# Low weight parts written over the raw tiles: four shared buffers in place of three raw and three low ones

## The reference, cut to what matters

```python
h = rmsnorm(x, norm_mix[i])
proj = h @ w_in[i]
...
merged = gates[:, :, 0] * y_attn + gates[:, :, 1] * y_conv + gates[:, :, 2] * y_ssm
x = x + merged @ w_mix_o[i]
h = rmsnorm(x, norm_ffn[i])
gt, up = jnp.split(h @ w_ffn_in[i], 2, axis=-1)
x = x + (jax.nn.silu(gt) * up) @ w_ffn_out[i]
```

## Time and profile before

| | |
|---|---|
| median of three runs | 2869.71 us (2868.93 to 2874.04) |
| the profiled execution | 2872.15 us, span 2870.4 us, mean granted TensorE clock 0.934 |
| TensorE matmul busy | 2582.4 us (90%), 12117 instructions |
| VectorE busy | 1469.2 us (51%) |
| ScalarE busy | 1034.8 us (36%) |
| GpSimd busy | 1023.8 us (36%) |
| weight stream queue | 200.96 MB, 21.1% of the DMA engines' time |

### The profile page before, as it was taken

One profiled execution on the slowest core, in us unless ns is written; L12 is line 12 of the kernel. 1 busy time (PEld: TensorE's weight loads), 2 busy tenths in 40 slices (PEclk: granted clock), 3 DMA queues, 4 the chain that ended last, 5 costly groups with the idle time before them and its releaser, 6 DMA issues.

```text
span 2870.4 us, 31814 instructions
## 1 busy us (share of the span) xinstructions
PE 2582.4 (90%) x12117; PEld 2051.8 (71%) x12117; DVE 1469.2 (51%) x2304; ACT 1034.8 (36%) x1674; POOL 1023.8 (36%) x577
## 2 busy tenths in 40 slices
PE   4987999999999998898999999987976888799998
PEld 3776667878888777676878888875744466588887
DVE  7775443443344476643433252345588863554333
ACT  3323663332222422465232222352344563422221
POOL 3212333444444422233444444441222233244443
PEclk9999999999999999899999999997977589799999
DMA  3221222322232322122322222231100001122222
GB/s 132 72 67 41 74 70 77 103 89 96 96 103 83 95 77 57 60 69 68 98 103 99 99 96 96 88 112 66 66 8 1 1 12 55 52 81 97 97 100 81
DMA packets 80135, 217.97 MB, mean 76 GB/s; under 512 B 15728, under 2 KB 25328, under 8 KB 79472
## 3 DMA queue, kind: packets, MB, share of 16 engines
q1 hardware_dynamic: 60912, 200.96, 21.1%
q10 hardware_dynamic: 19072, 14.98, 2.0%
HBM read 207.25 MB, written 2.10 MB: 73 GB/s over the span
## 4 chain that ended last, share of the span: by engine, by line
PE 73%; DVE 20%; ACT 3%; issue 3%; POOL 1%; ACTq 0%; DMA 0%; DVEq 0%
PE psG L836 21%; PE psG L837 21%; PE psG L838 21%; DVE work_m L1668 2%; DVE work_b L1668 2%; DVE tmp L1668 2%; PE psO L1002 2%; DVE stats L1948 1%; DVE b_lo L1668 1%; DVE work_b L1671 1%; DVE work_b L2066 1%; DVE max L2065 1%; DVE b_hi L1679 1%; PE psO L1068 1%; PE psT L946 1%
## 5 line engine op out<-in xcount | busy, mean ns | idle before, releaser
L782 POOL TENSOR_TENSOR w_lo<-w_raw,w_hi 128x1024 fp32r<-128x1024 f32 (+4 forms) x417 | 919.7, 2209 | 1610.8 <-ACT w_hi L1260 1610.8
L836 PE MATMUL psG<-h_hi,w_hi 128*128 128x512 f32 x1944 | 785.6, 404 | 23.3 <-DVE h_lo L1712 17.4
L837 PE MATMUL psG<-h_lo,w_hi 128*128 128x512 f32 x1944 | 769.8, 396 | 0.0
L838 PE MATMUL psG<-h_hi,w_lo 128*128 128x512 f32 x1944 | 767.9, 395 | 0.0
L1260 ACT ACTIVATE w_hi<-w_raw 128x1024 fp32r<-128x1024 f32 (+4 forms) x417 | 404.8, 971 | 532.0 <-PE psG L838 514.5
L836 PEld LDWEIGHTS psG<-h_hi,w_hi 128*128 128x128 f32 x1944 | 373.1, 192 | 126.1 <-issue 33.7
L838 PEld LDWEIGHTS psG<-h_hi,w_lo 128*128 128x128 f32 x1944 | 372.6, 192 | 80.1
L837 PEld LDWEIGHTS psG<-h_lo,w_hi 128*128 128x128 f32 x1944 | 373.2, 192 | 77.6 <-issue 3.0
L1668 DVE TENSOR_TENSOR x<-x,psG 128x512 f32<-128x512 f32 x112 | 77.1, 688 | 432.3 <-PE psG L838 432.3
L836 PE MATMUL psG<-m_hi,w_hi 128*128 128x512 f32 x736 | 287.3, 390 | 1.8 <-DVE m_lo L1668 1.7
L837 PE MATMUL psG<-m_lo,w_hi 128*128 128x512 f32 x736 | 286.4, 389 | 0.0
(11 more groups left out here) (273 smaller groups left out, 2943.0 us busy)
## 6 DMA issues: line engine op xcount, KB each, us to landing
w_raw<-wstream SPq DMA_DIRECT2D x327, 512.0 KB, 3.3
w_raw<-wstream SPq DMA_DIRECT2D x64, 256.0 KB, 2.6
w_raw<-wstream SPq DMA_DIRECT2D x16, 384.0 KB, 3.0
work_b<-work_b ACTq DMA_DIRECT2D x16, 256.0 KB, 4.4
work_b<-cmpw ACTq DMA_DIRECT2D x2, 2048.0 KB, 7.7
x<-xT SPq DMA_DIRECT2D x4, 512.0 KB, 6.3
small_work<-ssmp ACTq DMA_DIRECT2D x8, 256.0 KB, 2.7
outT<-x SPq DMA_DIRECT2D x1, 2048.0 KB, 6.3
```

The lines of the kernel that those rows point to most:

```text
L782: pool.tensor_tensor(lo, w, hi.bitcast(F32), ALU.subtract).then_inc(s_split, 1)
L836: pe.matmul(out, whi, hi, start=(k == 0), stop=False)
L837: pe.matmul(out, whi, lo, start=False, stop=False)
L838: ins = pe.matmul(out, wlo, hi, start=False, stop=(k == K - 1))
```

## The change

The tensor `w_lo` is placed at the address of `w_raw`, and both have four slots. GpSimd subtracts the high part from the raw tile and writes the result over it. SP may load into a slot only when the product that reads the low part there has ended, so its wait goes to `s_job` of product n-4 in place of `s_split` of tile n-3. The high part keeps three slots. The pipeline has 28 KB a partition in place of 36, and all tensors placed after it move down by 8 KB.

```diff
--- before.py
+++ after.py
@@ -50,7 +50,7 @@
 UNITS_SW = 16
 XHEADS = 4
 
-RAW_SLOTS = 3
+RAW_SLOTS = 4
 SPLIT_SLOTS = 3
 GEMM_BANKS = 3
 
@@ -446,9 +446,9 @@
         Bl, _ = place("b_lo", [P, 12, SEQ], F32R)
         R, _ = place("work_m", [P, 2 * KD * SEQ], F32, at=m_at)
         R2, _ = place("work_b", [P, 24 * SEQ], F32, at=b_at)
-        raw, _ = place("w_raw", [P, RAW_SLOTS, 8 * P], F32)
+        raw, raw_at = place("w_raw", [P, RAW_SLOTS, 8 * P], F32)
+        Wl, _ = place("w_lo", [P, RAW_SLOTS, 8, P], F32R, at=raw_at)
         Wh, _ = place("w_hi", [P, SPLIT_SLOTS, 8, P], F32R)
-        Wl, _ = place("w_lo", [P, SPLIT_SLOTS, 8, P], F32R)
         CON, _ = place("consts", [P, CONST_N], F32)
         PAR, _ = place("params", [P, npar], F32)
         sqr, _ = place("squares", [P, 2, SEQ], F32)
@@ -761,7 +761,7 @@
                 sp_eng.dma_start(X[:, 2 * i:2 * i + 2, :], xT[:, 2 * i:2 * i + 2, :]).then_inc(s_x[i], 16)
             for n, (key, K, N, who) in enumerate(weights):
                 if n >= RAW_SLOTS:
-                    sp_eng.wait_ge(s_split, n - RAW_SLOTS + 1)
+                    sp_eng.wait_ge(s_job, n - RAW_SLOTS + 1)
                 src = wstream[offset[key]:offset[key] + K * P * P].rearrange("(p f) -> p f", p=P)
                 sp_eng.dma_start(raw[:, n % RAW_SLOTS, 0:K * P], src).then_inc(s_raw[n % RAW_SLOTS], 16)
                 if n == 1:
@@ -777,7 +777,7 @@
                 key, K, N, who = weights[n]
                 w = raw[:, n % RAW_SLOTS, 0:K * P]
                 hi = Wh[:, n % SPLIT_SLOTS, 0:K, :].rearrange("p k n -> p (k n)")
-                lo = Wl[:, n % SPLIT_SLOTS, 0:K, :].rearrange("p k n -> p (k n)")
+                lo = Wl[:, n % RAW_SLOTS, 0:K, :].rearrange("p k n -> p (k n)")
                 pool.wait_ge(s_hi, n + 1)
                 pool.tensor_tensor(lo, w, hi.bitcast(F32), ALU.subtract).then_inc(s_split, 1)
 
@@ -832,7 +832,7 @@
                     hi, lo = moving(key, k)
                     for need in h_need(key, k):
                         pe.wait_ge(*need)
-                    whi, wlo = Wh[:, w % SPLIT_SLOTS, k, :], Wl[:, w % SPLIT_SLOTS, k, :]
+                    whi, wlo = Wh[:, w % SPLIT_SLOTS, k, :], Wl[:, w % RAW_SLOTS, k, :]
                     pe.matmul(out, whi, hi, start=(k == 0), stop=False)
                     pe.matmul(out, whi, lo, start=False, stop=False)
                     ins = pe.matmul(out, wlo, hi, start=False, stop=(k == K - 1))
```

## The result

The changed kernel takes 2894.67 us (median of four runs, 2887.29 to 2899.67), the kernel before 2870.52 us in the four runs beside it (2868.93 to 2874.04). The ratio is 1.008, with a 95% interval of 1.0056 to 1.0104. In a later session the same two kernels gave 2888.51 and 2875.35 us, ratio 1.0052 (1.0035 to 1.0069). So the forecast of no change, 2870.7, was wrong, and the median lies above the range's upper end, 2880.

What follows compares the result with a forecast made beforehand. TensorE's products were taken to set the end, with VectorE in the state-space stage. Projections +0.3 and state-space +0.7 gave +1.0 us: 2873.2 for the profiled execution, 2870.7 for the median, range 2863 to 2880.

Steps and rivals of the forecast that it cites:

- The release rule: Weight loads everywhere: load n goes when product n-4 has ended, no longer when split n-3 is done.
- Feed-forward, outputs and last stage at 0: Feed-forward, mix and output products: loads still land ahead of rounding, 2.1 us for eight-block tiles; cost 0.
- Gates: late 33 us in all, cost 0: Gates and their outputs: eight-block tiles land 0.5 to 1.0 us late, 48 times, absorbed by 4.1 us of cover.
- rival A: Eight-block roundings after four-block products: ScalarE's wait for raw tiles slows the kernel, 2885 us, or 2904 without cover; chance 0.08.
- the 45 that the prediction allowed: Gate stages: ScalarE's new wait for the DMA at eight-block tiles, some 48 times, under 45 us in all.
- In place and addresses at 0: GpSimd's subtraction in place and the addresses moved down by 8 KB a partition: each taken as 0.
- Projections +0.3: Projections of the second block: three tiles late by 0.1 to 0.6 us, cost 0 to +1.3, taken as +0.3 us.
- State-space stages +0.7: State-space stages: moved loads collide with the last Toeplitz copies, at most 1.4 us a group, partly halved: +0.7 us.
- the sum of full collisions, +5.2: State-space stages: upper bound with all five new collisions of loads and copies counted in full, +5.2 us.
- rival B: State-space stages: loads collide with copies in full, 2876 us, above it if the delayed VectorE chain meets splits; chance 0.07.
- rival C: Start of the mix products: a late split lets VectorE's cast through, 4.2 us gained, 2866.5, at best 2863; chance 0.10.
- the two that the forecast gave no slack: State-space stages: two of six groups whose copies VectorE waits for, said to have no slack, at most 1.4 us each.

Runs made afterwards that it cites:

- separate-buffer kernel: The kernel before, its three raw and three low buffers kept, where SP also waits for product n-4 before load n: 2892.33 us, ratio 1.0066.
- the kernel with the right loads held: The changed kernel with eight loads (tiles 8, 12, 16, 20, 157, 161, 165, 169) held until their group's Toeplitz copies landed: 2873.57 us, ratio 1.001.

## Why the prediction was wrong

*The release rule* was right. SP waits for the product (2721.0 us, 413 times).

*Feed-forward, outputs and last stage at 0*: right. The shift stays at +13.0 to +13.3 from the gates of layer 0 to product 155, and at +27.5 through the last stage. The load of tile 112 went out at 753.57, after product 108's end at 753.54.

*Gates: late 33 us in all, cost 0*: right. The idle time ahead of the rounding grew by 28.7 us. One pair, from the timelines of SP, ScalarE, GpSimd and TensorE of the changed kernel:

```profile
514.47 0.33 SPq L766 DMA_DIRECT2D w_raw<-wstream  x1
...
518.02 1.06 ACT L1260 ACTIVATE w_hi<-w_raw 128x1024 fp32r<-128x1024 f32 x1 [2.19 <-DMA w_raw<-wstream]
...
519.16 2.39 POOL L782 TENSOR_TENSOR w_lo<-w_raw,w_hi 128x1024 fp32r<-128x1024 f32 x1 [1.96 <-ACT w_hi L1260]
...
525.15 0.39 PE L836 MATMUL psG<-h_hi,w_hi 128*128 128x512 f32 x1
```

Against the earlier trace rows, product 64's end is 13.28 us later (501.16 to 514.44), the rounding 14.04, the split's start 14.04, and the product at the end, 525.15, again 13.27: the 0.76 us of delay is gone. So rival A was wrong, as its small chance said. The wait's sum, 64.3 us, is above the 45 that the prediction allowed, because idle time already there is counted in.

*In place and addresses at 0*: right as far as the intervals tell, by the separate-buffer kernel (1.0066 without either, 1.008 and 1.0052 with both).

*Projections +0.3*: missed in size. They cost 6.6 us in the first profile, and little of it lies in the close chain of ScalarE, which waits there for raw tiles three times, 1.4 us in all. TensorE's work from the start of product 322 to that of 323 takes 8.4 us at a granted clock of 0.69 (2050.3 to 2058.7), where it took 6.0 at 1.00 (2026.5 to 2032.5). TensorE's idle stretches in the approach are of the same length in both kernels, 4.93 and 1.95 us. In the second profile of the same changed kernel product 321 has no step and 323 has 1.6 us, and in the separate-buffer kernel neither has one. This part varies from run to run, and stays open below.

*State-space stages +0.7*: **this is the step that failed.** The place was right, and the price of one collision too (1.7 us measured between copies of 1.8 and 3.5 us; I had 1.4). Two things were wrong in it. First, I halved the price because a load issued shortly ahead of the last copy would have few packets under way. It went out 0.02 us ahead, and the delay came in full in the first group, 1.77 us; of the eight groups the closest pair cost the copy most (3.5 us), and the copies of 2.5 to 2.7 us had the load 1.5 to 1.7 us ahead. The Trainium skill, "DMA: Bandwidth & Descriptors", in the section on queues, rings and completion order, which has each DMA engine go round-robin between its queue rows packet by packet, was nearer: all six groups that VectorE waits for collide, each copy by 0.7 to 1.7 us. But the sum of full collisions, +5.2, falls short as well, by a factor of three to four: the two stages cost 22 us in one profile and 17 in the other. Second and above all, I let a delay of VectorE pass one to one to the end. The chain is not a row of fixed durations. The timing of three splits against it decides whether an instruction takes 0.3, 0.7 or 1.2 us, or some two microseconds more, and whether TensorE idles 1.6 or 5.9 us, hence at which clock it goes on. In the two large steps 1.8 us became 6.65, and 1.1 us became 7.1.

This is the mechanism of rival B, "when the delayed VectorE chain also meets splits", to which the forecast gave 0.07 and no price above 2876. The rows to price it were read: a cast of 0.43 us that takes 2.50 beside a split. They were used for rival C, a gain, and not for the chain that the same text called the bound. Had I laid the delayed chain over the splits, whose instants hardly move (93.19 before, 93.31 after), it would have shown two instructions of 1024 columns held up in place of one. And the trace of before had the outcome in it: TensorE idled 4.1 to 7.9 us at L946 in five groups, and 1.6 and 0 in the two that the forecast gave no slack.

The Trainium skill, "SBUF — State Buffer", in the section on SBUF's two sides, has the shared port held for a whole instruction by whichever comes first, a VectorE operation with two inputs in SBUF or a GpSimd operation. The rows agree: an instruction that starts 0.14 us after a split takes 3.30 us in place of 1.23, and ends 1.08 us after the split does, which is about its own length.

**Rival C** had the other sign of the same effect. Its gain in the mix products did not come: the cast there, at 551.96, takes 2.50 us again. But a gain of 34 us was there to be had from the same rule, by waiting on purpose.

## What stays open

What sets the clock in the projections, the keys and the attention: between the kernels run here, and between two profiles of the same changed kernel, product 321 comes 3.1 us later or not at all, and the keys give back 1.6 or 3.1. The step at 321 and 323 goes with the granted clock, after idle stretches of equal length. Which of the instants before decides was not tried. It is worth up to 6 us of the 27.5, and may be why the two comparisons gave 1.008 and 1.0052.

Why the load and the last copy fall together in every group was read from the instants only; no run moved the copies.

## What to carry to other kernels

When a change only moves an instant, price the move by laying the delayed chain over its neighbours, GpSimd's two-input instructions above all: slack and one-to-one delays are not enough where a row shows one operation at two durations. A buffer shared with the low part ties loads to the ends of products; here such an end fell within 1.8 us ahead of a small, urgent copy in every one of eight groups, so look for what else is in flight at those instants. If GpSimd has slack, let its large subtractions wait until the VectorE result that TensorE needs is out: here that was worth 34 us, and with it the smaller buffers cost nothing that could be told.

## What was not expected of the hardware

A copy of 8 KB beside a load of 512 KB took 3.5 us in place of 1.8, as long as the load itself (3.3 us). TensorE's granted clock was 0.50 for 4.9 us after 5.87 us of idleness, so that waiting cost 2.4 us on top of itself; after 4.13 us, in the kernel with the right loads held, it was 0.50 as well; after 1.61 us it was 1.00. And a delay of 1.6 us on VectorE, with nothing else changed, cost 6.5 and 7.2 us.
